# The down projection of a SwiGLU layer as seven block products, set between the gate and up products

## The chip, the cores and the metric

The kernel runs on one core of a Trainium2 chip. The metric is the device time of one execution in microseconds. The kernel before the change takes 1409.84 us, the median of 3 runs (1408.72 to 1411.44). It computes one layer of a transformer in float32: 1024 tokens, model width 1024, feed-forward width 2816.

## The reference

The layer is a causal stick-breaking attention with 16 heads of 64, beside it a cross attention of 4 heads over 256 memory rows, an output projection with residual, and then the part that the change touches:

```python
def rms_norm(x, g):
    xf = x.astype(jnp.float32)
    y = xf * lax.rsqrt(jnp.mean(xf * xf, axis=-1, keepdims=True) + EPS)
    return (y * g.astype(jnp.float32)).astype(x.dtype)

def swiglu(h, w_gate, w_up, w_down):
    return (jax.nn.silu(h @ w_gate) * (h @ w_up)) @ w_down
...
        x = x + jnp.concatenate([mix, cross], axis=-1) @ w_out[i]
        x = x + swiglu(rms_norm(x, ffn_norm[i]), w_gate[i], w_up[i], w_down[i])
```

The result must have float32's accuracy. TensorE reads float32 operands in a shortened form, so the kernel splits each operand into a high part (a copy in that form, name ending in h) and a low part (the operand minus its high part, name ending in l), and sums three matrix products: high by high, high by low, low by high. A "split" below is this pair: ScalarE writes the high part, another engine subtracts for the low part.

## The kernel before, in words

The feed-forward width is cut into 11 chunks of 256 (two blocks of 128, called fb). For a chunk the kernel computes gate and up, transposed, as 256 x 1024; then the block silu(gate) * up (called gu, also 256 x 1024, kept as four pieces of 128 x 512: fb by half of the tokens); then the product of gu with the chunk's 256 rows of w_down, which is added to the residual x2 (1024 x 1024, in SBUF for the whole stage).

Gate and up are already computed with seven block products each (Strassen's method in Winograd's form). Each such product is a `pe_product`: 12 matmuls of 128 x 512 output (4 blocks of the contracted width times 3 of the split), into PSUM banks 4 to 7. The sums of weight blocks that they need are made by GpSimd (`pool_sums`, four operations for each of gate and up), their high parts by ScalarE (`act_part_high`), their low parts by VectorE (`dve_part_low`). ScalarE copies products that are needed twice out of PSUM (`act_keep`), VectorE adds products (`dve_sum`) and forms the block from them (`dve_block`, with ScalarE's sigmoid before it).

The down product (`pe_down`) is done in the plain way: 8 token tiles by 2 column halves, for each 6 matmuls into one of the banks 0 to 3 in turn, and after each VectorE adds that bank to x2 (`dve_down`, 128 x 512). The 256 x 1024 rows of w_down arrive in two halves of 512 KB and are split by ScalarE and VectorE in operations of 128 x 1024 (`act_down_w`, `dve_down_w`). The gu block is split piece by piece (`act_block_high`, `dve_block_low`).

One pass of the program (`pe_body` and the functions of the same form for the other engines) computes the gate products of chunk c + 1, the down product of chunk c, and the up products of chunk c + 1. The first chunk's gate and up are made before, in the plain way (`pe_first`), and among them stand TensorE's transposes of the second half of the tokens (`pe_turn`, banks 0 and 1 in turn, copied out by `act_second` and `dve_second`). There are 10 passes: one written out, a loop with 4 turns of two, and one more written out. The last chunk's down product stands alone behind them. Nothing is scheduled by a planner: the order on each engine is the order of the calls in these functions, each engine runs its own in that order, and semaphores carry the dependencies.

Of the kernel before, what the change touches and what calls it, by code (L numbers as in the profile page):

```python
# [19 lines left out]
def trunk(nc, x, mem, norms, w_mem_kv, w_out, w_gate, w_up, w_down, sb_w_in, out):  # L20
# [35 lines left out]
    with ExitStack() as ctx:  # L56
# [22 lines left out]
        own = take("own", [P, BANK // 2 + 1], BF16, BANK + 2)  # L79
# [46 lines left out]
        pv_low = take("pv_low", [P, 2 * P])  # L126
        KB = 1024
        ex_at = cursor[0]
        cursor[0] += 14 * KB
        assert cursor[0] <= nc.sbuf_usable_end  # L130
# [46 lines left out]
        gu_h = at("gu_h", [P, FB, S], F32R, mk_at)  # L177
        gu_at = (x_at + 32 * KB - 2 * ROW, raw_at)
        gu_x = [at(f"gu_x{b}", [P, FB, S], F32, gu_at[b]) for b in range(2)]
        gu_l = [at(f"gu_l{b}", [P, FB, S], F32R, gu_at[b]) for b in range(2)]  # L180
# [22 lines left out]
        dw_at = (h_at, h_at + 16 * KB)  # L203
        dw_h = [at(f"dw_h{n}", [P, FB, BANK], F32R, dw_at[n]) for n in range(2)]
        dw_x = [at(f"dw_x{n}", [P, FB, BANK], F32, dw_at[n] + ROW) for n in range(2)]
        dw_l = [at(f"dw_l{n}", [P, FB, BANK], F32R, dw_at[n] + ROW) for n in range(2)]
# [427 lines left out]
        s_fd = [sem("down_w_left_loaded"), sem("down_w_right_loaded")]  # L634
        s_dh = sem("down_w_high_done")
        s_dl = sem("down_w_low_done")
# [447 lines left out]
        def act_first_high(act, half, fb):  # L1084
            n = 2 * half + fb
            act.wait_ge(s_bl, n + 1)
            c = slice(half * BANK, (half + 1) * BANK)
            act.activation(gu_h[:, fb, c], gu_x[0][:, fb, c], ACT.Copy).then_inc(s_gh, 1)

        def dve_first(dve, half, fb):  # L1090
            n = 2 * half + fb
            g = gu_x[0][:, fb, half * BANK:(half + 1) * BANK]
# [5 lines left out]

        def dve_first_low(dve, half, fb):
            n = 2 * half + fb  # L1100
            g = gu_x[0][:, fb, half * BANK:(half + 1) * BANK]
            c = slice(half * BANK, (half + 1) * BANK)
            dve.wait_ge(s_gh, n + 1)
            dve.tensor_tensor(gu_l[0][:, fb, c], g, gu_h[:, fb, c].bitcast(F32), ALU.subtract).then_inc(s_gl, 1)

# [69 lines left out]
        G0 = 8  # L1175
        DOWN_LAST = tuple(range(NT // 2, NT)) + tuple(range(NT // 2))
# [42 lines left out]
        def pool_sums(pool, c, m):  # L1219
# [9 lines left out]
            pool.tensor_tensor(a21, a11, a21, ALU.subtract).then_inc(s_sc, 1)  # L1229
            part_loaded(pool, c, m, 1)  # L1230
# [61 lines left out]
        def act_keep(act, c, m, i):  # L1292
# [31 lines left out]
        def dve_block(dve, c, m, par, i):  # L1324
            g, k = block_of(gu_x[par], i), kept[KEPT_OF[i]][:, :]
# [87 lines left out]
        def act_body(act, c, par, first=False, ahead=True):  # L1413
# [6 lines left out]
            if not first:  # L1420
                act_sigmoid(act, g, par1, 0)
# [538 lines left out]
```

## Time and profile before

| | |
|---|---|
| median of 3 runs | 1409.84 us |
| the profiled execution's own time | 1409.1 us |
| its span, first to last instruction | 1407.3 us |
| granted TensorE clock, mean | 0.993 |
| TensorE (PE) busy | 1365.0 us, 97% |
| VectorE (DVE) busy | 948.7 us, 67% |
| ScalarE (ACT) busy | 655.8 us, 47% |
| GpSimd (POOL) busy | 186.6 us, 13% |
| moved by DMA | 69.94 MB, mean 50 GB/s |

The profile is of one execution, whose span lies 1.8 us under its own device time. Matmul records overlap each other: a record lasts about 0.39 us, but the next matmul starts about 0.23 us after the one before. So TensorE's pace is read from start to start, or from the length of a stretch and the number of matmuls in it, not from the length of a record. VectorE's records overlap too: 128 x 512 operations of 0.69 us follow each other after 0.60 us. In the names, "x" is x2, "ps" is PSUM, L12 is line 12 of the kernel before.

### The profile page before, as it was taken

Reading aid. Unit: us, or ns where it says so; the run is one execution under the profiler, and the core shown is the slowest. Engines: PE = TensorE matmul, PEld = TensorE weight load, DVE = VectorE, ACT = ScalarE, POOL = GpSimd, SP = SyncE. Lnnn points to the kernel's source line nnn. Section 1 sums busy time; section 2 is a strip of 40 time slices with the busy share of each in tenths; the row PEclk is TensorE's granted clock in tenths of the full one; section 3 lists DMA queues with packets and bytes.
Section 4 is the critical chain, followed back from the end, with each engine's and each line's share of the span. In section 5 each row is a group of like instructions: output and inputs, shape, how many; then the busy total and the mean of one; then the engine's idle time right before and its main releaser. Section 6 shows DMA issues by size and latency. Waiting matters only on the chain. (4 is left out here: it accounts for less than half of the span.)

```text
span 1407.3 us, 20453 instructions
## 1 busy us (share of the span) xinstructions
PE 1365.0 (97%) x6974; PEld 1115.6 (79%) x6974; DVE 948.7 (67%) x1344; ACT 655.8 (47%) x1124; POOL 186.6 (13%) x155
## 2 busy tenths in 40 slices
PE   7999999999999999599999999999999999999999
PEld 4777888787888888488887788888888888888887
DVE  6677979788797978795257856556564555756455
ACT  7566666656666665762253422324133241322321
POOL 0000000000000000214015211202111121111200
PEclk9999999999999999799999999999999999999999
DMA  6100100101010011105111211111111111121103
GB/s 240 31 24 23 31 24 23 30 22 30 22 30 23 22 31 31 45 24 162 41 30 31 81 55 45 45 61 45 60 60 45 52 37 61 43 66 52 45 31 135
DMA packets 90118, 69.94 MB, mean 50 GB/s; under 512 B 3792, under 2 KB 75472, under 8 KB 90064
## 3 DMA queue, kind: packets, MB, share of 16 engines
q1 hardware_dynamic: 90064, 69.23, 15.9%
q8 instruction: 32, 0.52, 0.2%
q14 instruction: 22, 0.18, 0.0%
HBM read 65.03 MB, written 4.19 MB: 49 GB/s over the span
## 5 line engine op out<-in xcount | busy, mean ns | idle before, releaser
L1394 DVE TENSOR_TENSOR x<-ps,x 128x512 f32<-128x512 f32 x176 | 121.6, 691 | 71.2 <-PE ps L1384 67.0
L1300 ACT ACTIVATE kept<-ps 128x512 f32<-128x512 f32 x60 | 35.7, 595 | 235.4 <-PE ps L1288 235.4
L438 ACT ACTIVATE a_h<-ps 128x256 fp32r<-128x256 f32 (+2 forms) x96 | 78.0, 812 | 136.9 <-PE ps L353 136.9
L315 PE MATMUL ps<-hh,w_h 128*128 128x512 f32 x336 | 140.3, 417 | 0.0
L1384 PE MATMUL ps<-dw_h,gu_l 128*128 128x512 f32 x352 | 138.5, 394 | 0.0
L1384 PE MATMUL ps<-dw_l,gu_h 128*128 128x512 f32 x352 | 137.5, 391 | 0.0
L1384 PE MATMUL ps<-dw_h,gu_h 128*128 128x512 f32 x352 | 137.0, 389 | 0.3 <-issue 0.3
L315 PE MATMUL ps<-hh,w_l 128*128 128x512 f32 x336 | 132.4, 394 | 0.0
L315 PE MATMUL ps<-hl,w_h 128*128 128x512 f32 x336 | 131.9, 393 | 0.0
L1288 PE MATMUL ps<-ft_h,part_l 128*128 128x512 f32 x320 | 126.5, 395 | 0.0
L1288 PE MATMUL ps<-ft_l,part_h 128*128 128x512 f32 x320 | 125.2, 391 | 0.0
L1288 PE MATMUL ps<-ft_h,part_h 128*128 128x512 f32 x320 | 124.5, 389 | 0.0
L547 DVE TENSOR_TENSOR a_l<-ps,a_h 128x256 fp32r<-128x256 f32 (+2 forms) x96 | 91.6, 954 | 48.7 <-ACT a_h L438 48.1
L521 DVE TENSOR_TENSOR_SCAN fail<-fail,own 128x129 f32<-128x129 f32 (+3 forms) x128 | 107.8, 870 | 0.0
L1258 DVE TENSOR_TENSOR part_l<-part_x,part_h 128x512 fp32r<-128x512 f32 x140 | 94.4, 691 | 5.3 <-ACT part_h L1251 2.8
L534 DVE TENSOR_TENSOR succ<-fail,succ 128x256 f32<-128x256 f32 (+2 forms) x96 | 94.7, 987 | 0.3
L1288 PE MATMUL ps<-f_h,part_l 128*128 128x512 f32 x240 | 94.7, 395 | 0.0
L353 PE MATMUL ps<-ident,succ 128*128 128x128 f32 x576 | 81.4, 278 | 13.5 <-DVE a_l L547 8.6
L1288 PE MATMUL ps<-f_h,part_h 128*128 128x512 f32 x240 | 93.5, 390 | 0.6 <-DVE part_l L1258 0.6
L1288 PE MATMUL ps<-f_l,part_h 128*128 128x512 f32 x240 | 93.8, 391 | 0.0
L1312 DVE TENSOR_TENSOR kept<-ps,kept 128x512 f32<-128x512 f32 x30 | 20.8, 692 | 104.0 <-PE ps L1288 104.0
L554 POOL TENSOR_TENSOR o_t<-o_t,pv_low 128x256 f32 x24 | 23.7, 988 | 476.8 <-ACT o_t L450 476.8
(219 smaller groups left out, 3120.4 us busy)
## 6 DMA issues: line engine op xcount, KB each, us to landing
w_raw<-in_sb_w_in SPq DMA_DIRECT2D x52, 256.0 KB, 2.9
dw_x<-in_w_down SPq DMA_DIRECT2D x22, 512.0 KB, 3.3
part_x<-in_w_gate SPq DMA_DIRECT2D x40, 256.0 KB, 3.5
part_x<-in_w_up SPq DMA_DIRECT2D x40, 256.0 KB, 2.9
wo_raw<-in_w_out SPq DMA_DIRECT2D x20, 256.0 KB, 2.8
x_in<-in_x SPq DMA_DIRECT2D x8, 512.0 KB, 7.8
x<-in_x SPq DMA_DIRECT2D x16, 256.0 KB, 6.0
out<-x SPq DMA_DIRECT2D x16, 256.0 KB, 2.0
```

The lines of the kernel that those rows point to most:

```text
L315: mm = pe.matmul(j_ps[:, 0], w[:, kc // 4, kc % 4], h[:, kc, half * BANK:(half + 1) * BANK], start=(kc == 0 and i == 0), stop=(kc == KC - ...
L353: mm = pe.transpose(t_ps[:, h, j * P:(j + 1) * P], succ[:, u % 2, h, j * P:(j + 1) * P], ident[:, :])
L438: act.activation(a_h[:, :, 0:w // P, col * P:(col + 1) * P], t_ps[:, :, 0:w].rearrange("p h (j q) -> p h j q", q=P), ACT.Copy).then_inc(s_ ...
L521: dve.tensor_tensor_scan(back, back, own[:, BANK - w:BANK + 1][:, ::-1], 0.0, ALU.mult, ALU.max).then_inc(s_scan, 1)
L534: done = dve.tensor_tensor(g, f[:, :, 1:w + 1], g, ALU.mult)
L547: dve.tensor_tensor(a_l[:, :, 0:w // P, c], t_ps[:, :, 0:w].rearrange("p h (j q) -> p h j q", q=P), a_h[:, :, 0:w // P, c].bitcast(F32), A ...
L554: pool.tensor_tensor(both, both, pv_low[:, :], ALU.add).then_inc(s_o, 1)
L1258: dve.tensor_tensor(part_l[m][p][:, :, :].rearrange(flat), part_x[m][p][:, :, :].rearrange(flat), part_h[p][:, :, :].rearrange(flat).bitca ...
L1288: mm = pe.matmul(product_bank(m, p), w[:, k], g[:, k], start=(p in (0, 1, 3) and k == 0 and i == 0), stop=(k == 3 and i == 2), skip_group_ ...
L1300: act.activation(kept[i][:, :], product_bank(m, (0, 2, 3)[i]), ACT.Copy).then_inc(s_kp, 1)
L1384: mm = pe.matmul(ps[:, (2, 3, 0, 1)[d % 4]], g[:, fb, t * P:(t + 1) * P], w[n][:, fb], start=(fb == 0 and i == 0), stop=(fb == FB - 1 and ...
L1394: dve.tensor_tensor(o, ps[:, (2, 3, 0, 1)[d % 4]], o, ALU.add).then_inc(s_x2, 1)
```

## The change

Each down product except the last chunk's becomes seven block products of the same method. With A the transposed gu block (its pieces A11, A12, A21, A22) and B the chunk's rows of w_down (pieces B11 to B22 of 128 x 512), product k is one of seven combinations of A times one of seven combinations of B: 4 token tiles by 3 of the split, 12 matmuls, each tile into a bank of its own, banks 0 to 3. The products accumulate in the banks, and start anew at k = 0, 4 and 5. After each one VectorE adds all four banks to a quarter of x2 in one operation of 128 x 4 x 512 (`dve_down`), and TensorE may not begin the next one before that add is done.

The seven stand between the 14 gate and up products, one behind every second. GpSimd makes the sums of A (`pool_a_sum`, four) and of B (`pool_b_sum`, four) and the seven low parts of B (`pool_b_low`); ScalarE makes 14 high parts (`act_a_high`, `act_b_high`), VectorE seven low parts of A (`dve_a_low`), each 128 x 512. High and low parts lie in rings of two. w_down arrives in four pieces of 256 KB for each chunk. `pool_sums` is cut, its last sum now stands apart (`pool_last_sum`).

The last chunk keeps the plain way (`pe_last`), now with eight banks in turn. Silu keeps its two steps (gate times sigmoid before, times up afterwards). The transposes among the first chunk's products rotate through banks 0 to 3 (`turn_ps`, `wait_turn_bank`). The diff, cut to what the text speaks of:

```diff
+            if g >= XU0 + KC:
+                return ps[:, (g - XU0 - KC) % 4]
-            if g >= XU0:
+            if g in (XU0 + KC + 2, XU0 + KC + 3):
+                pe.wait_ge(s_x2, X0)
+            elif g >= XU0 + KC + 4:
+                pe.wait_ge(s_xl, g - 3)
+            elif g >= XU0:
                 pe.wait_ge(s_xl, g - 1)
...
+        A_OPS = (A11, "S2", "S3", "A22", "A12", S1, S4)
+        B_OPS = ("B11", "B11", "B12", "B12", "B21", "B11", "B22")
+        C_OF = ((0, 0), (0, 1), (1, 1), (1, 0), (0, 0), (1, 1), (0, 1))
+
+        def ring_free(act, c, k):
+
+            if k >= 2 or not (isinstance(c, int) and c == 0):
+                act.wait_ge(s_dn, down_done(c, k - 2) if k >= 2 else down_done(c - 1, k + 5))
+
+        def act_a_high(act, c, par, k):
+            ring_free(act, c, k)
+            if k in (0, 3, 4):
+                act.wait_ge(s_bl, block_done(c, {0: 0, 3: 1, 4: 3}[k]))
+            else:
+                act.wait_ge(s_as, 4 * c + {1: 2, 2: 3, 5: 1, 6: 4}[k])
+            act.activation(ah[(par + k) % 2][:, :], ax[a_slot(par, A_OPS[k])][:, :], ACT.Copy).then_inc(s_gh, 1)
+
+        def a_low(par, k):
+            return al[a_slot(par, A_OPS[k]) if k else "low of A11"]
+
+        def dve_a_low(dve, c, par, k):
+
+            dve.wait_ge(s_gh, 7 * c + k + 1)
+            if 0 < k < 6:
+                dve.wait_ge(s_as, 4 * c + (0, 4, 3, 1, 4, 2)[k])
+            slot = a_slot(par, A_OPS[k])
+            dve.tensor_tensor(a_low(par, k)[:, :], ax[slot][:, :], ah[(par + k) % 2][:, :].bitcast(F32), ALU.subtract
+                              ).then_inc(s_gl, 1)
+
+            if n == 0:
+                pool.wait_ge(s_bd["B12"], 16 * c + 16)
+                pool.wait_ge(s_bd["B22"], 16 * c + 16)
+                pool.tensor_tensor(b12, b22, b12, ALU.subtract).then_inc(s_bs, 1)
+            elif n == 1:
+                pool.wait_ge(s_bs, 4 * c + 1)
+                pool.wait_ge(s_bw, 7 * c + 1)
+                pool.tensor_tensor(b11, b12, b11, ALU.add).then_inc(s_bs, 1)
...
+        def pool_b_low(pool, c, par, k):
+            pool.wait_ge(s_bh, 7 * c + k + 1)
+            pool.tensor_tensor(bl[(par + k) % 2][:, :], bx[B_OPS[k]][:, :], bh[(par + k) % 2][:, :].bitcast(F32),
+                               ALU.subtract).then_inc(s_bw, 1)
+
+        def pe_down(pe, c, par, k):
+
+            pe.wait_ge(s_gl, 7 * c + k + 1)
+            pe.wait_ge(s_bw, 7 * c + k + 1)
+            h, l = ah[(par + k) % 2], a_low(par, k)
+            wh, wl_ = bh[(par + k) % 2], bl[(par + k) % 2]
+            pe.wait_ge(s_x2, X0 + 7 * c + k)
+            for t in range(4):
+                for i, (g, w) in enumerate(((h, wh), (h, wl_), (l, wh))):
+                    mm = pe.matmul(ps[:, t], g[:, t * P:(t + 1) * P], w[:, :], start=(k in (0, 4, 5) and i == 0),
+                                   stop=(i == 2), skip_group_check=True)
+            mm.then_inc(s_dn, 1)
+
+        def dve_down(dve, c, k):
+            half, n = C_OF[k]
+            d = 7 * c + k
+            dve.wait_ge(s_dn, d + 2)
+            dve.wait_ge(s_x2, X0 if isinstance(c, int) and c == 0 and k < 2 else X0 + d - 1)
+            o = x2[:, 4 * half:4 * half + 4, n * BANK:(n + 1) * BANK]
+            dve.tensor_tensor(o, ps[:, 0:4], o, ALU.add).then_inc(s_x2, 1)
+
+
...
-            for p in range(7):
-                pe_product(pe, c + 1, 0, p)
-            pe_down(pe, c, par)
-            for p in range(7):
-                pe_product(pe, c + 1, 1, p)
+            after = (1, 3, 5, 7, 9, 11, 13)
+            for n in range(14):
+                pe_product(pe, c + 1, n // 7, n % 7)
+                if n in after:
+                    pe_down(pe, c, par, after.index(n))
+
+        def pool_body(pool, c, par, ahead=True):
+            pool_a_sum(pool, c, par, 3)
+            pool_b_low(pool, c, par, 1)
+            pool_b_low(pool, c, par, 2)
+            pool_b_sum(pool, c, 2)
+            pool_b_sum(pool, c, 3)
+            pool_sums(pool, c + 1, 1)
+            pool_b_low(pool, c, par, 3)
+            pool_last_sum(pool, c + 1, 1)
+            for k in (4, 5, 6):
+                pool_b_low(pool, c, par, k)
+            if ahead:
+                pool_sums(pool, c + 2, 0)
+                pool_b_sum(pool, c + 1, 0)
+                pool_b_low(pool, c + 1, 1 - par, 0)
+                pool_last_sum(pool, c + 2, 0)
+                pool_b_sum(pool, c + 1, 1)
+                for n in range(3):
+                    pool_a_sum(pool, c + 1, 1 - par, n)
 
...
```

**What moves, in the engines' order.** TensorE in the first pass before the change, at the end of the seventh gate product (L1288) and the start of the down product (L1384); part_h and part_l are parts of the gate weights, dw_h and dw_l of w_down, gu_h and gu_l of the block:

```order
L1288 MATMUL ps<-ft_h4_153,part_h6_192 128x512
L1288 MATMUL ps<-ft_l4_157,part_h6_192 128x512
L1288 MATMUL ps<-ft_h4_153,part_l06_178 128x512
L1384 MATMUL ps<-dw_h0_193,gu_h_139 128x512
L1384 MATMUL ps<-dw_l0_197,gu_h_139 128x512
L1384 MATMUL ps<-dw_h0_193,gu_l0_142 128x512
```

TensorE in the first pass after the change, at the end of the second gate product (L1298) and the first down product (L1478), whose rows repeat four times; bh and bl are parts of B, ah of A:

```order
L1298 MATMUL ps<-f_h0_130,part_h1_202 128x512
L1298 MATMUL ps<-f_l0_132,part_h1_202 128x512
L1298 MATMUL ps<-f_h0_130,part_l01_188 128x512
L1478 MATMUL ps<-bh0_212,ah0_157 128x512
L1478 MATMUL ps<-bl0_214,ah0_157 128x512
L1478 MATMUL ps<-bh0_212,al_low of A11_156 128x512
```

The down product has moved from behind seven gate products to behind the second, and there are 12 of its matmuls there where 96 stood in one piece.

VectorE in the loop before the change, at the last gate piece and the first adds of the down product (L1394); kept0 and kept1 are products copied out of PSUM:

```order
L1328 TENSOR_TENSOR gu_x0_140<-gu_x0_140,kept1_200 128x512
L1255 REGISTER_ALU
L1258 TENSOR_TENSOR part_l11_180<-part_x11_166,part_h1_187 128x512
L1327 REGISTER_ALU
L1328 TENSOR_TENSOR gu_x0_140<-ps,kept0_199 128x512
L1391 ISA
L1392 REGISTER_ALU
L1394 TENSOR_TENSOR x2_124<-ps,x2_124 128x512
L1255 REGISTER_ALU
L1258 TENSOR_TENSOR part_l12_181<-part_x12_167,part_h2_188 128x512
L1391 REGISTER_ALU
L1394 TENSOR_TENSOR x2_124<-ps,x2_124 128x512
L1255 REGISTER_ALU
```

VectorE in the first pass after the change, from the add of down product 0 to that of product 1 (L1488); A22 here holds S2, one of the sums of A, and the rows at L1389 are low parts of A:

```order
L1488 TENSOR_TENSOR x2_124<-ps,x2_124 128x4x512
L1389 TENSOR_TENSOR A22_152<-A22_143,ah1_158 128x512
L1268 TENSOR_TENSOR part_l04_191<-part_x04_177,part_h4_205 128x512
L1268 TENSOR_TENSOR part_l05_192<-part_x05_178,part_h5_206 128x512
L1334 TENSOR_TENSOR ax_A11_139<-ps,kept0_228 128x512
L1268 TENSOR_TENSOR part_l06_193<-part_x06_179,part_h6_207 128x512
L1350 TENSOR_TENSOR ax_A11_139<-ax_A11_139,kept0_228 128x512
L1389 TENSOR_TENSOR al_A21_149<-ax_A21_140,ah0_157 128x512
L1488 TENSOR_TENSOR x2_124<-ps,x2_124 128x4x512
```

Between two adds of a bank stood at most one other operation; now two adds of four banks have seven operations between them, six of which read no PSUM (in the loop the first of them stands ahead of the first add).

GpSimd in the loop before the change, the four sums for the up weights:

```order
L1224 ISA
L1225 TENSOR_TENSOR part_x13_168<-part_x14_169,part_x16_171 128x512
L1198 REGISTER_ALU
L1227 ISA
L1228 TENSOR_TENSOR part_x12_167<-part_x13_168,part_x10_165 128x512
L1229 TENSOR_TENSOR part_x14_169<-part_x10_165,part_x14_169 128x512
L1231 REGISTER_ALU
L1236 TENSOR_TENSOR part_x15_170<-part_x11_166,part_x12_167 128x512
```

GpSimd in the loop after the change, from the low part of B's product 1 to the sums for the up weights (part_x12 to part_x14):

```order
L1466 TENSOR_TENSOR bl1_215<-bx_B11_208,bh1_213 128x512
L1465 REGISTER_ALU
L1466 TENSOR_TENSOR bl0_214<-bx_B12_209,bh0_212 128x512
L1449 TENSOR_TENSOR bx_B12_209<-bx_B21_210,bx_B11_208 128x512
L1451 REGISTER_ALU
L1452 TENSOR_TENSOR bx_B11_208<-bx_B22_211,bx_B11_208 128x512
L1231 REGISTER_ALU
L1232 TENSOR_TENSOR part_x13_183<-part_x14_184,part_x16_186 128x512
L1234 REGISTER_ALU
L1235 TENSOR_TENSOR part_x12_182<-part_x13_183,part_x10_180 128x512
L1236 TENSOR_TENSOR part_x14_184<-part_x10_180,part_x14_184 128x512
```

The up sums stand behind four operations for the down product that were not on this engine; a pass holds 23 operations where it held 8.

## Rows read from the trace of the kernel before

**Rows 1.** The chain that ended last, in order of time: start us, us, what.

```profile
771.97 1.25 POOL part_x L1229
...
775.09 19.64 PE ps L1288 x84
794.73 22.19 PE ps L1384 x96
816.91 38.62 PE ps L1288 x168
855.54 21.77 PE ps L1384 x96
...
1381.39 0.30 issue
1381.69 22.44 PE ps L1384 x96
```

**Rows 2.** PE's waits from 690 us on: line, released by, us in total, times, longest.

```profile
PE ps L719 <- DVE ft_x L1129: 2.0, 1, 2.0
PE ps L1288 <- DVE part_l L1258: 0.6, 1, 0.6
```

**Rows 3.** Busy us (instructions) by stretch: length, PE PEld DVE ACT POOL, granted clock.

```profile
998.52:1119.72 121.20, 121.20 (x529) 99.12 (x529) 69.42 (x100) 35.80 (x60) 20.62 (x16) 1.00 0.17 52
775.09:1381.39 606.30, 606.30 (x2640) 495.63 (x2640) 353.59 (x503) 180.79 (x301) 99.44 (x76) 1.00 0.17 51
```

**Rows 4.** Groups of two passes (998.52 to 1119.72 us): busy us, mean ns; idle before.

```profile
L1394 DVE TENSOR_TENSOR x<-ps,x 128x512 f32<-128x512 f32 x32 | 22.1, 691 | 12.4 <-PE ps L1384 11.6
L1258 DVE TENSOR_TENSOR part_l<-part_x,part_h 128x512 fp32r<-128x512 f32 x28 | 18.7, 684 | 0.6 <-ACT part_h L1251 0.6
L1251 ACT ACTIVATE part_h<-part_x 128x512 fp32r<-128x512 f32 x28 | 16.0, 621 | 2.4 <-POOL part_x L1228 2.4
L1225 POOL TENSOR_TENSOR part_x<-part_x,part_x 128x512 f32<-128x512 f32 x4 | 5.2, 1296 | 93.9 <-PE ps L1288 93.9
```

**Rows 5.** Timeline of VectorE, 1133 to 1141 us: start us, us.

```profile
1133.58 0.69 DVE L1312 TENSOR_TENSOR kept<-ps,kept 128x512 f32<-128x512 f32 x1 [5.31 <-PE ps L1288]
1134.31 1.04 DVE L1335 TENSOR_TENSOR gu_x<-kept,gu_x 128x512 f32<-128x512 f32 x1
...
1138.73 1.88 DVE L1258 TENSOR_TENSOR part_l<-part_x,part_h 128x512 fp32r<-128x512 f32 x3
```

**Rows 6.** Timeline of GpSimd, the same stretch.

```profile
1133.51 1.29 POOL L1229 TENSOR_TENSOR part_x<-part_x,part_x 128x512 f32<-128x512 f32 x1
```

**Rows 7.** Timeline of VectorE from 786 us on.

```profile
786.89 2.32 DVE L1368 TENSOR_TENSOR dw_l<-dw_x,dw_h 128x1024 fp32r<-128x1024 f32 x1
```

**Rows 8.** Timeline of GpSimd, the same stretch.

```profile
788.26 2.09 POOL L1228 TENSOR_TENSOR part_x<-part_x,part_x 128x512 f32<-128x512 f32 x1
```

**Rows 9.** The 128x2048 add, timeline of VectorE.

```profile
764.96 2.29 DVE L1154 TENSOR_TENSOR f<-f,ft_x 128x2048 f32<-128x2048 f32 x1 [1.19 <-POOL f L1148]
```

**Rows 10.** GpSimd's in-place sums at L1148: ns least, median, longest.

```profile
L1148 POOL TENSOR_TENSOR f<-f,f x4: 1318/2556/3352, 755.3 to 761.6; 128x512 f32<-128x512 f32 x4
```

**Rows 11.** The page's DMA issues: KB each, median us to landing.

```profile
part_x<-in_w_up SPq DMA_DIRECT2D x40, 256.0 KB, 2.9
```

**Rows 12.** Timeline of PE among the first chunk's products.

```profile
740.59 0.66 PE L719 MATMUL ps<-ident,xn 128*128 128x128 f32 x4 [0.47 <-DVE ft_x L1126]
...
742.25 0.40 PE L1068 MATMUL ps<-f_h,gw_l 128*128 128x512 f32 x1
744.60 1.11 PE L719 MATMUL ps<-ident,xn 128*128 128x128 f32 x4 [1.96 <-DVE ft_x L1129]
...
748.03 0.39 PE L1068 MATMUL ps<-f_h,gw_h 128*128 128x512 f32 x1
```

**Rows 13.** The granted clock behind the second wait, columns as in Rows 3.

```profile
744.60:748.00 3.40, 3.40 (x10) 2.89 (x11) 3.37 (x6) 0.69 (x1) 0.00 (x0) 0.50 0.00 0
```

**Rows 14.** Timeline of GpSimd before the first pass.

```profile
768.99 1.28 POOL L1225 TENSOR_TENSOR part_x<-part_x,part_x 128x512 f32<-128x512 f32 x1 [4.06 <-DMA part_x<-in_w_gate]
```

More of the change, by code:

```diff
@@ L1371, in pe_down, with block_done @@
-        def pe_down(pe, c, par, last=False):
+        def block_done(c, i):
+            return (1, 4, 3, 2)[i] if isinstance(c, int) and c == 0 else blocks(c, 1, i + 1)
+        A_OPS = (A11, "S2", "S3", "A22", "A12", S1, S4)
[4 more added lines that the diff above has]
+                act.wait_ge(s_dn, down_done(c, k - 2) if k >= 2 else down_done(c - 1, k + 5))
@@ L1382, in pe_down @@
[L1382 to L1392 removed]
+                    pe.wait_ge(s_gl, 7 * LAST + 3)
+                elif d == NT // 2:
+                    pe.wait_ge(s_gl, 7 * LAST + 4)
@@ new lines, in pe_last @@
+                if d == 3:
+                    pe.wait_ge(s_bl, blocks(LAST, 1, 4))
+                elif d > 3:
+                    pe.wait_ge(s_x2, X0 + DN * LAST + max(0, d - 7))
+                for fb in range(FB):
+                    i = BLOCKS.index((fb, half))
+                    h, l = last_ah[i], al[a_slot(0, (A11, "A22", A21, "A12")[i])]
+                    for j, (g, w) in enumerate(((h, last_bh), (h, last_bl), (l, last_bh))):
+                        mm = pe.matmul(last_bank(d), g[:, q], w[n][fb][:, :],
+                                       start=(fb == 0 and j == 0), stop=(fb == FB - 1 and j == 2))
@@ L1393, in dve_down, with dve_last @@
+                mm.then_inc(s_dn, 1)
+        def dve_last(dve, d):
+            n, t = d // NT, DOWN_LAST[d % NT]
+            dve.wait_ge(s_dn, DN * LAST + d + 2)
+            dve.wait_ge(s_x2, X0 + DN * LAST)
             o = x2[:, t, n * BANK:(n + 1) * BANK]
-            dve.tensor_tensor(o, ps[:, (2, 3, 0, 1)[d % 4]], o, ALU.add).then_inc(s_x2, 1)
+            dve.tensor_tensor(o, last_bank(d), o, ALU.add).then_inc(s_x2, 1)
         def sp_body(sp, c, ahead=True):
-            for n in (2, 3, 0, 1):
+            first = isinstance(c, int) and c == 0
+            for n in (2, 3):
@@ L1444, in act_body @@
                     act_part_high(act, g + 1, 0, p)
-            for i in range(1, 4):
-                act_block_high(act, g, par1, i)
+                act_b_high(act, g, par1, 0)
+                act_a_high(act, g, par1, 0)
         def dve_body(dve, c, par, first=False, ahead=True):
@@ L1720, in _ @@
             act_body(act, FC - 2, 1, ahead=False)
-            act_down_w(act, FC - 1, 1)
+            act_last_a(act, 0)
+            act_last_a(act, 1)
+            act_last_b(act, 0, 0)
+            act_last_a(act, 2)
+            act_last_b(act, 0, 1)
+            act_last_a(act, 3)
+            for fb in range(FB):
+                act_last_b(act, 1, fb)
         @block.vector
@@ L1849, in _ @@
             for d in range(2 * NT):
[L1850 to L1852 removed]
+                dve_last(dve, d)
         @block.tensor
```

334 lines of the change are left out of this document (204 added, 130 removed).

## The prediction, made before the changed kernel had run

> **What bounds the kernel now.** First the chain of waits: from 775.09 us to the end it is TensorE alone, in a strict pattern: 96 matmuls of the down product in 21.77 or 22.19 us, then 168 gate and up matmuls, ten times, and the last chunk's 96 at the end [rows 1]. Then PE's waits: after 690 us there are two worth a word, 2.0 and 0.6 us, both ahead of the first pass; inside the passes none [rows 2]. Then busy time by stretch: the ten passes take 606.30 us and hold 2640 matmuls, so 0.2297 us each and 60.63 us a pass, at clock 1.00; over two passes VectorE is busy 69.42 of 121.20 us, ScalarE 35.80, GpSimd 20.62 [rows 3]. The passes cost what their matmuls cost. So a matmul less is worth 0.23 us as long as the other engines, which get more work, stay in time.
>
> **The matmuls.** A down product has 7 x 12 = 84 instead of 96: 12 less in each of ten passes, 120 x 0.2297 = 27.6 us off. The new ones have the shape of the old. Between the two lengths of the old down product the pace differs by 0.0044 us, 0.4 us a pass in either direction; I take the mean. The new pass is 252 x 0.2297 = 57.9 us. I call the gate and up products P0 to P13 and the down products D0 to D6; each is 12 matmuls, 2.76 us, in the order P0 P1 D0 P2 P3 D1 P4 P5 D2 P6 P7 D3 and so on.
>
> **The load of the others, per pass.** VectorE loses 16 adds at 0.691, four low parts of 0.69 and two of 1.2 us, and gets seven low parts and seven adds of 2048 columns. The trace has no such add out of PSUM. One of 512 columns out of PSUM takes 0.691 us, as long as one within SBUF (0.684), and one of 2048 columns within SBUF 2.29 [rows 4, 9]; three low parts in a row take 1.88, so 0.60 from start to start [rows 5]. Ends: 2.2 (the same 0.09 overlapped) and 2.4 (four times 0.60); I take 2.29, the row of its size. Sum: 34.7 - 11.1 - 2.8 - 2.4 + 4.8 + 16.0 = 39 of 57.9 us. ScalarE loses two of 1.06 and four of 0.63 and gets 14 of 0.62: 22 us. GpSimd goes from 8 to 23 operations of 1.30: 30 us [rows 3, 4]. w_down comes in pieces of 256 KB; such a piece lands in 2.9 us [rows 11], and each is asked for when its buffer's last low part is made, 8 us or more before its use; SP's queue holds nothing that waits longer than these. Cost nothing; were one late, GpSimd's sum behind it would be late by as much.
>
> **What the engines cost each other.** At 1134.31 VectorE begins a product of two SBUF tiles while GpSimd runs from 1133.51 to 1134.80; it takes 1.04 us instead of 0.69, ending 0.55 us after GpSimd did. The add out of PSUM at 1133.58 under the same GpSimd operation takes its plain 0.69 [rows 5, 6]. The other way round, GpSimd's sum at 788.26 takes 2.09 us, with VectorE in a low part until 789.21 [rows 7, 8]. So a GpSimd operation and a VectorE operation with two SBUF inputs exclude each other for their whole length; PSUM operands are free of it.
> The Trainium skill has this as a rule (SBUF — State Buffer, section on SBUF's two separate sides): the pair of ports is an exclusive lock, and the loser blocks fully. By this rule, the trace agrees (1.04 for 0.69 us). It speaks against this change, which nearly triples GpSimd's operations; the sum by it is the 1384 below; if the two only shared bandwidth, there would be no queueing in the passes, and it would be 1381.
> In a pass 27 VectorE operations have two SBUF inputs (14 + 7 low parts, 6 block steps): 27 x 0.60 = 16 us, beside GpSimd's 30: 46 of 57.9 us, if never idle together. It fits, so only a local rush can stall TensorE.
>
> **Where it is tight.** TensorE may start Dk when the add of D(k-1) is done, 5.5 us after it ended; the add takes 2.3, so VectorE may be 3.2 us late. The worst place is D2. From the end of D0 to the start of D2 TensorE has P2 P3 D1 P4 P5, 13.8 us. VectorE has in that time, in this order: the add of D0 (2.2), two part_l, a sum, part_l, a block step, a low part of A (six times 0.60), then the add of D1 (2.3): 8.1 us. GpSimd has there two sums of B and the three up sums, which may start at the end of P3; five operations of 1.3 us, 6.5 us, and I find nearly each of them ahead of one waiting VectorE operation. 8.1 + 6.5 = 14.6, less what GpSimd does under the first add and the sum, about 1.1, plus hand-overs between engines of some 0.05 us each: 13.9 to 14.2. So D2 is 0.1 to 0.4 us late; I take 0.3. Ends: 0 (GpSimd finds its gaps) and 1.7 us (nothing overlaps, eight hand-overs of 0.1). The other places, walked the same way, keep over 1.8 us (D0 of the next pass, behind the three A sums) or over 2 us (D3, P6, P7). Ten passes: 3 us, ends 0 and 17.
>
> **Ahead of the first pass.** Two transposes of the second half wait for a bank, 0.47 and 1.96 us [rows 2, 12], and the matmuls behind the second run at clock 0.50, the lower level of 1.2 GHz, after that idle time, until 748.03 [rows 12, 13]: one group of transposes and six matmuls in 3.4 us where 1.9 would do. With four banks both waits go: 0.5 + 2.1 + 1.5 = 4.1 us. What is late next is P0: it waited 0.57 us already on the low part of the first gate weights, whose DMAs wait for GpSimd's f sums, and these for the last of the same transposes. So that chain moves up too. GpSimd's new low part of B falls into its 4.06 us wait for the DMA [rows 14], VectorE's low part of 2048 columns now stands ahead of the first part_l and may cost some tenths. I take 3.8 off; ends 0 and 4.1.
> In the first pass D1 needs all four sums of A and two of B, and these the last block, 1.4 us into P0: seven GpSimd operations (9.1), VectorE's three part_l and one operation of 2048 columns between them (4), ScalarE's high part (0.6): 15.1 us, against 13.8: 1.3 late. The backlog makes D2 late again, about 1.5. 2.8 us on, ends 0 and 5.
>
> **The end.** D6 now stands behind the last up product, so the last block's split hides behind it: the 0.3 us gap ahead of the last 96 matmuls goes [rows 1]; these stay.
>
> **Sum**, against the profiled execution's 1409.1 us (span 1407.3 and 1.8 around it): 1409.1 - 27.6 - 3.8 + 2.8 + 3.0 - 0.3 = 1383.2. The median of the runs is 0.7 above that execution: **1384 us**.
>
> **Rivals.**
> (a) No stalls in the passes, and a full gain ahead of them: 1409.8 - 27.6 - 4.1 - 0.3 = 1378. For it: VectorE and GpSimd have a fifth of the time spare even if they exclude each other. Against: three up sums start just as VectorE has its densest row.
> (b) The rush at D2 costs the upper end, 1.7 us a pass: 1384 + 14 = 1398. For it: GpSimd's four in-place sums under VectorE's load had a median of 2.56 and up to 3.35 us instead of 1.32 [rows 10].
> (c) Slower. The same queueing, one step on: with GpSimd's operations at the 2.45 us which they average there, 23 fill 56 of 57.9 us, GpSimd's order becomes the pace and D2 waits as long as the transposes did, 2.1 us, and pulls the clock down once a pass, 1.5 us more. With 0.4 us for the pace behind it, 4.0 x 10 - 27.6 - 1.3 = +11: 1421. It decides from 2.9 us of stall a pass on (27.6 + 1.3 over ten). Against: the waits are bounded by the other's length, and VectorE's two-SBUF work is 16 us of 58, not the dense row of 2048-column operations as there.
> (d) The matmuls themselves go slower: each bank gets only three at a time, where the old down product put six into one. At 0.26 us for the 84, 2.5 us a pass come back: 1409. Against: the gate and up products add across products too, and run at 38.62/168 = 0.2299 [rows 1].
>
> **Chances.** Forecast 0.52, (a) 0.25, (b) 0.14, (c) 0.06, (d) 0.03. A change within 0.2% (2.8 us) can't be told from none here. Faster 0.91, the same 0.03, slower 0.06. The range reaches from (a) to just past (b): 1377 to 1400, with (c), (d) and a little beyond outside, some 1 in 7.
>
> **What would show it.** In the profile after: 252 matmuls a pass and a pass of 57.9 to 58.5 us; PE's waits on the down line, released by VectorE's add, at D2 before any other; no wait at the transposes and no stretch at 0.50; GpSimd near 30 us busy a pass (well above 35 would be (b) or (c)); the four-bank add at 2.3 us. It is wrong if PE's waits per pass exceed 1.7 us, if another semaphore (a DMA of w_down, a high part) ends them, or if the pace of the matmuls changes.

## The result and the profile after

| | before | after |
|---|---|---|
| median of the runs, us | 1409.64 (1408.72 to 1411.44) | 1386.13 (1384.76 to 1387.05) |
| ratio, 95% interval | | 0.9831 (0.9814 to 0.9848) |
| profiled execution: time, span, us | 1409.1, 1407.3 | 1385.98, 1384.2 |
| first to last product of the first chunk (to P0), us | 52.45 | 52.07 |
| P0 to the last 96 matmuls, us | 606.60 | 581.97 |

The kernel is 23.5 us faster; forecast were 1384 us and a range of 1377 to 1400. The last two lines are start times of PE's timeline taken from each other. Together they are 25.0 us shorter. The part ahead of them, whose code did not change but for the places of two small tiles (tested below), took 1.8 us longer in this execution: the first chunk's products start at 724.47 us, 722.64 before, and between 722.6 and 725.7 over all the kernels below. That is why small effects are read below from these two stretches beside the medians.

The page of the changed kernel, busy time by engine and the group of the new add:

```profile
PE 1339.9 (97%) x6854; PEld 1094.1 (79%) x6854; DVE 1083.0 (78%) x1262; ACT 689.2 (50%) x1206; POOL 424.1 (31%) x309
L1488 DVE TENSOR_TENSOR x<-ps,x 128x2048 f32<-128x2048 f32 x70 | 160.1, 2287 | 71.4 <-PE ps L1478 71.3
```

Its chain of waits, in order of time (start us, us, what), which answers to [rows 1]: the down product (L1478) is now 12 matmuls between pairs of gate and up products (L1298). Where some 2.7 us are missing between two rows of 24, a down product stood.

```profile
1011.17 5.55 PE ps L1298 x24
1016.71 2.77 PE ps L1478 x12
1019.49 5.55 PE ps L1298 x24
1027.77 5.50 PE ps L1298 x24
...
1358.67 22.36 PE ps L1533 x96
```

Busy time by stretch, columns as in [rows 3]: from D2 of the first pass to the end of the passes, all ten passes, and two passes in the middle.

```profile
801.36:1358.51 557.15, 557.15 (x2425) 455.23 (x2426) 461.77 (x409) 205.62 (x368) 309.38 (x215) 1.00 0.18 53
776.54:1358.51 581.97, 579.69 (x2522) 473.03 (x2521) 484.38 (x423) 216.61 (x386) 332.61 (x228) 1.00 0.18 54
1000.08:1115.98 115.90, 115.90 (x506) 94.71 (x505) 97.04 (x85) 42.45 (x76) 66.99 (x47) 1.00 0.18 54
```

From 801.36 us on PE is busy all the time, at clock 1.00; a pass takes 57.95 us. In it VectorE is busy 48.5 us, ScalarE 21.2, GpSimd 33.5. PE's waits after 690 us, answering to [rows 2]:

```profile
PE ps L1087 <- DVE ft_x L1134: 2.9, 1, 2.9
PE ps L1478 <- POOL bl L1466: 2.3, 1, 2.3
```

The first is new, in the first chunk. The second is D2 of the first pass. It starts at 801.36 us, 0.15 us after the add of D1 has ended, on which it waits (timeline of VectorE):

```profile
798.93 2.28 DVE L1488 TENSOR_TENSOR x<-ps,x 128x2048 f32<-128x2048 f32 x1
```

The low part that the view names, made at the same time, is the one for D3; in the kernels below the same wait stands with the add.

The place that was walked in the prediction, from the add of D0 to that of D1, here in a pass in the middle; timeline of VectorE, then GpSimd:

```profile
1019.61 2.29 DVE L1488 TENSOR_TENSOR x<-ps,x 128x2048 f32<-128x2048 f32 x1 [1.56 <-PE ps L1478]
1021.82 3.50 DVE L1268 TENSOR_TENSOR part_l<-part_x,part_h 128x512 fp32r<-128x512 f32 x2
1025.24 0.68 DVE L1334 TENSOR_TENSOR ax_A<-ps,kept 128x512 f32<-128x512 f32 x1
1025.85 1.18 DVE L1268 TENSOR_TENSOR part_l<-part_x,part_h 128x512 fp32r<-128x512 f32 x1
1026.95 1.78 DVE L1350 TENSOR_TENSOR ax_A<-ax_A,kept 128x512 f32<-128x512 f32 x1
1028.65 1.79 DVE L1389 TENSOR_TENSOR al_A<-ax_A,ah 128x512 fp32r<-128x512 f32 x1
1030.37 2.28 DVE L1488 TENSOR_TENSOR x<-ps,x 128x2048 f32<-128x2048 f32 x1
```

```profile
1021.78 1.29 POOL L1449 TENSOR_TENSOR bx_B<-bx_B,bx_B 128x512 f32<-128x512 f32 x1 [0.17 <-POOL bl L1466]
1023.16 1.61 POOL L1452 TENSOR_TENSOR bx_B<-bx_B,bx_B 128x512 f32<-128x512 f32 x1
1025.12 1.36 POOL L1232 TENSOR_TENSOR part_x<-part_x,part_x 128x512 f32<-128x512 f32 x1 [0.35 <-PE ps L1298]
1026.56 1.62 POOL L1235 TENSOR_TENSOR part_x<-part_x,part_x 128x512 f32<-128x512 f32 x1
1028.14 1.75 POOL L1236 TENSOR_TENSOR part_x<-part_x,part_x 128x512 f32<-128x512 f32 x1
```

Every VectorE operation with two SBUF inputs here is held until the GpSimd operation in progress has ended (1.2 to 1.8 us instead of 0.68, 3.50 instead of 1.29 for the two at 1021.82); the one that reads PSUM at 1025.24 keeps its 0.68, the two adds their 2.29. D2 starts at 1033.11, 0.5 us after the add has ended: it keeps up, with little to spare.

### The profile page after: what moved, and what is told of

It is laid out like the page before. It is cut to its first block, busy times and chain, and to the rows that moved or that the text cites. A ratio compares the mean times of both kernels' runs of the same rounds, so it can differ in the third digit from the quotient of the medians.

```text
span 1384.2 us, 20643 instructions
## 1 busy us (share of the span) xinstructions
PE 1339.9 (97%) x6854; PEld 1094.1 (79%) x6854; DVE 1083.0 (78%) x1262; ACT 689.2 (50%) x1206; POOL 424.1 (31%) x309
## 4 chain that ended last, share of the span: by engine, by line
PE 91%; ACT 3%; DVE 3%; POOL 2%; issue 1%; DMA 0%; SPq 0%; ACTq 0%; POOLq 0%; DVEq 0%
PE ps L1298 27%; PE ps L326 17%; PE ps L1478 14%; PE ps L1010 7%; PE ps L380 5%; PE ps L364 5%; PE ps L354 4%; PE ps L295 3%; PE ps L1087 2%; PE ps L1533 2%; PE ps L798 1%; ACT junk L703 1%; PE ps L938 1%; PE ps L902 0%; PE ps L738 0%
## 5 line engine op out<-in xcount | busy, mean ns | idle before, releaser
L1488 DVE TENSOR_TENSOR x<-ps,x 128x2048 f32<-128x2048 f32 x70 | 160.1, 2287 | 71.4 <-PE ps L1478 71.3
L1466 POOL TENSOR_TENSOR bl<-bx_B,bh 128x512 fp32r<-128x512 f32 x70 | 96.6, 1380 | 200.5 <-ACT bh L1462 200.5
L1268 DVE TENSOR_TENSOR part_l<-part_x,part_h 128x512 fp32r<-128x512 f32 x140 | 140.5, 1033 | 2.5 <-POOL part_x L1236 2.5
L558 DVE TENSOR_TENSOR a_l<-ps,a_h 128x256 fp32r<-128x256 f32 (+2 forms) x96 | 91.5, 953 | 48.9 <-ACT a_h L449 48.5
L1298 PE MATMUL ps<-ft_h,part_l 128*128 128x512 f32 x320 | 126.5, 395 | 0.0
L1298 PE MATMUL ps<-ft_l,part_h 128*128 128x512 f32 x320 | 125.2, 391 | 0.0
L1298 PE MATMUL ps<-ft_h,part_h 128*128 128x512 f32 x320 | 124.5, 389 | 0.0
L1478 PE MATMUL ps<-bh,ah 128*128 128x512 f32 x280 | 109.1, 390 | 2.3 <-POOL bl L1466 2.3
L1478 PE MATMUL ps<-bl,ah 128*128 128x512 f32 x280 | 109.5, 391 | 0.0
L364 PE MATMUL ps<-ident,succ 128*128 128x128 f32 x576 | 82.0, 279 | 13.3 <-DVE a_l L558 8.6
L1298 PE MATMUL ps<-f_h,part_l 128*128 128x512 f32 x240 | 94.7, 395 | 0.0
L1261 ACT ACTIVATE part_h<-part_x 128x512 fp32r<-128x512 f32 x140 | 82.9, 621 | 22.9 <-POOL part_x L1235 14.2
L1298 PE MATMUL ps<-f_l,part_h 128*128 128x512 f32 x240 | 93.9, 391 | 0.0
L1298 PE MATMUL ps<-f_h,part_h 128*128 128x512 f32 x240 | 93.4, 389 | 0.0
```

The costliest lines, as they stand in the source:

```text
L364: mm = pe.transpose(t_ps[:, h, j * P:(j + 1) * P], succ[:, u % 2, h, j * P:(j + 1) * P], ident[:, :])
L558: dve.tensor_tensor(a_l[:, :, 0:w // P, c], t_ps[:, :, 0:w].rearrange("p h (j q) -> p h j q", q=P), a_h[:, :, 0:w // P, c].bitcast(F32), A ...
L1261: act.activation(part_h[p][:, :, :].rearrange(flat), part_x[m][p][:, :, :].rearrange(flat), ACT.Copy).then_inc(s_fh, 1)
L1268: dve.tensor_tensor(part_l[m][p][:, :, :].rearrange(flat), part_x[m][p][:, :, :].rearrange(flat), part_h[p][:, :, :].rearrange(flat).bitca ...
L1298: mm = pe.matmul(product_bank(m, p), w[:, k], g[:, k], start=(p in (0, 1, 3) and k == 0 and i == 0), stop=(k == 3 and i == 2), skip_group_ ...
L1466: pool.tensor_tensor(bl[(par + k) % 2][:, :], bx[B_OPS[k]][:, :], bh[(par + k) % 2][:, :].bitcast(F32), ALU.subtract).then_inc(s_bw, 1)
```

## The experiments

Times are medians; the kernel before, on the same chips, had 1409.6. "Chunk" is from the first chunk's first product to P0, "passes" from P0 to the last 96 matmuls, each in the profiled execution; "turns" are the transposes of the second half of the tokens.

| kernel | us (ratio to before, 95%) | chunk | passes | sum |
|---|---|---|---|---|
| before | 1409.6 | 52.45 | 606.60 | 659.05 |
| after | 1386.13 (0.981 to 0.985) | 52.07 | 581.97 | 634.04 |
| before, turns in four banks | 1412.95 (1.0014 to 1.0036) | 55.53 | 606.49 | 662.02 |
| before, two tiles moved | 1410.08 (0.9993 to 1.0012) | 52.43 | 606.60 | 659.03 |
| after, turns in two banks | 1385.97 (0.9822 to 0.9849) | 50.63 | 582.21 | 632.84 |
| after, sums late | 1386.29 (0.9821 to 0.9848) | 50.89 | 583.77 | 634.66 |
| after, f sums wait | 1387.99 (0.9832 to 0.9862) | 54.03 | 582.20 | 636.23 |
| after, four adds | 1387.86 (0.9829 to 0.9856) | 51.89 | 582.15 | 634.04 |
| after, one more | 1388.24 (0.9830 to 0.9862) | 52.07 | 583.53 | 635.60 |
| after, three more | 1395.52 (0.9882 to 0.9915) | 52.04 | 591.02 | 643.06 |
| after, 12 matmuls back | 1410.74 (1.0000 to 1.0018) | 53.25 | 608.19 | 661.44 |
| after, up sums late | 1385.44 (0.9817 to 0.9844) | 52.06 | 580.96 | 633.02 |
| after, three edits | 1383.45 (0.9805 to 0.9831) | 49.06 | 582.87 | 631.93 |

**Is the gain the matmuls?** Down product 0 of each pass is made twice:

```diff
-            for t in range(4):
+            for t in (0, 1, 2, 3, 0, 1, 2, 3) if k == 0 else range(4):
```

> The 12 matmuls of down product 0 are made twice in each of the ten passes (the second time over the first), so a down product has 96 matmuls again in the new order. Theory (the gain of the change is the 120 matmuls, at 0.2297 us each): 27.6 us come back, less what of the 2.4 us wait of the first pass the later D1 and D2 hide: 1411.3 to 1413.7. Rival (a part of the gain is the new order or the four banks at once): under 1410.

1410.74: the gain is gone, though the median lies under the range of the theory and over that of the rival. The two stretches are 27.4 us longer for 120 matmuls. The wait at D2 of the first pass is 1.2 us shorter (1.1 for 2.3), as PE's waits of this kernel show:

```profile
PE ps L1478 <- DVE x L1488: 1.1, 1, 1.1
```

And the low clock behind the wait of the first chunk holds for six more matmuls, 1.2 us longer. So the new order, the adds of four banks and three matmuls at a time in a bank are worth nothing by themselves: with 96 matmuls they leave the stretches 2.4 us longer than before, by the waits of the chunk and of the first pass.

**Where the data lie.** Two tiles of an earlier stage change places in SBUF in the kernel before, as in the changed kernel.

> The kernel before, with only the two small tiles own and pv_low at their new places in SBUF. In the changed kernel's trace the first matmul of the first chunk starts at 724.47 us, in the kernel before at 722.64. Theory 1 (that 1.8 us is the spread between executions): 1409.6 within 1 us, that start anywhere from 722 to 725. Theory 2 (the places of the tiles cost it): 1411.4 and a start near 724.5.

Nothing, to 0.1%. In this kernel the first chunk's products start at 723.93 us, where they started at 722.64 before and at 724.47 after: inside the spread, as the first theory had it.

**The transposes.** Only the four banks, on the kernel before; and the changed kernel with the two banks of before:

```diff
+            if g >= XU0 + KC:
+                return ps[:, (g - XU0 - KC) % 4]
...
-            if g >= XU0:
+            if g in (XU0 + KC + 2, XU0 + KC + 3):
+                pe.wait_ge(s_x2, X0)
+            elif g >= XU0 + KC + 4:
+                pe.wait_ge(s_xl, g - 3)
+            elif g >= XU0:
```

> The kernel before, with only the four banks for the eight transposes among the first chunk's products. Theory 1 (what stalls TensorE there is VectorE's chain that copies the eight tiles out, and more banks only move the wait to the first product that needs all of them, the first matmul of the second half): the two waits at the transposes (0.5 and 2.0 us) go, a wait of 1.5 to 3 us with matmuls at clock 0.50 behind it appears on the first chunk's own matmuls, released by VectorE; the time is 0 to 1.5 us under the kernel before. Theory 2 (my prediction's step: the banks are what is waited for): no such wait, 3.8 us less, 1405.8.

> The changed kernel, with the transposes back in two banks in turn. Theory 1: the wait of 2.9 us on the first chunk's matmuls turns back into one of about 2 us at the transposes; the time is within 1 us of the changed kernel's 1386.1. Theory 2: 3.8 us more, 1390.

Alone on the kernel before, the four banks make it slower, 3.1 us in the chunk and 3.4 by the medians; in the changed kernel they cost 1.4 us in the chunk, which the medians don't show. The waits at the transposes do go in both. PE's waits after 690 us with the four banks alone:

```profile
PE ps L1074 <- DVE ft_x L1135: 5.9, 1, 5.9
PE ps L1390 <- issue: 0.3, 1, 0.3
```

PE has only run ahead: the first product of the second half needs all eight transposes copied out by VectorE. And the earlier last transpose releases GpSimd's eight f sums, which now run beside VectorE's copies. In the changed kernel (timelines of VectorE, GpSimd and PE) three of VectorE's four sums take 1.55 us instead of 0.69, then PE starts, and at the lower clock:

```profile
745.06 0.69 DVE L1137 TENSOR_TENSOR ft_x<-ft_x,f 128x512 f32<-128x512 f32 x1
...
747.11 1.55 DVE L1137 TENSOR_TENSOR ft_x<-ft_x,f 128x512 f32<-128x512 f32 x1
```

```profile
746.82 5.89 POOL L1149 TENSOR_TENSOR f<-f_h,f_l 128x512 f32<-128x512 f32 x4 [28.82 <-PE ps L738]
```

```profile
753.06 0.77 PE L1087 MATMUL ps<-f_h,gw_h 128*128 128x512 f32 x1 [2.87 <-DVE ft_x L1134]
753.62 0.63 PE L1087 MATMUL ps<-f_l,gw_h 128*128 128x512 f32 x1
```

```profile
753.06:756.54 3.48, 3.48 (x8) 2.80 (x9) 1.50 (x2) 2.02 (x2) 3.48 (x3) 0.51 0.02 5
```

With two banks in the changed kernel these f sums start 1.5 us later, counted from the chunk's first product, and the second waiting transpose waits 0.60 us where it waited 1.96 before [rows 12]. What the traces show as the reason is another part of the change: before, ScalarE's high part of the first block stood between these copies and waited 2.80 us for VectorE, and VectorE's low part of it (0.69 us) stood between them too; now both stand behind them. No run moves these two alone. ScalarE's timeline before:

```profile
741.89 0.63 ACT L1088 ACTIVATE gu_h<-gu_x 128x512 fp32r<-128x512 f32 x1 [2.80 <-DVE gu_x L1097]
```

PE's waits of the changed kernel with two banks:

```profile
PE ps L1292 <- DVE part_l L1262: 1.4, 1, 1.4
PE ps L732 <- DVE ft_x L1128: 0.6, 1, 0.6
PE ps L732 <- DVE ft_x L1125: 0.5, 1, 0.5
```

**Is it the holding?** The f sums wait until VectorE is done, nothing else:

```diff
             pool.wait_ge(s_xt, XU0 + 2 * KC)
+            pool.wait_ge(s_ts, 4)
```

> GpSimd's eight f sums begin only when VectorE has made the last of its four sums of the second half; no more. Theory (with four banks the transposes end sooner, GpSimd's sums begin sooner and hold VectorE's three sums at 1.55 us instead of 0.69): PE's wait ahead of the first product of the second half falls from 2.9 us to 0.5 or less, without a stretch at the lower clock behind it; but GpSimd's sums begin some 5 us later, so the first gate weights come later and P0 starts 52 to 55 us behind the first product of the first chunk (52.1 in the changed kernel): 1386 to 1389. Rival (VectorE's queue of evictions is simply that long): the wait stays over 2 us, and the same time.

The four sums take 0.69 us again; PE's wait falls from 2.87 to 1.13 us, no matmul behind it is slow, and P0 waits 5.1 us instead, with twelve slow matmuls behind:

```profile
PE ps L1299 <- DVE part_l L1269: 5.1, 1, 5.1
PE ps L1087 <- DVE ft_x L1134: 1.1, 1, 1.1
```

So 1.7 us of the wait were the holding (the two of the three held sums that stand ahead of the last copy, 0.87 each) and 1.1 are VectorE's queue. My bound of 0.5 was too low; that the loss only changes its place came as expected. Taking the four sums together behind the copies does the same more gently:

```diff
-                dve.wait_ge(s_xl, XU0 + KC + c + 1)
-                dve.tensor_tensor(ft_x[2][:, k], ft_x[3][:, k], f11[:, k], ALU.add).then_inc(s_ts, 1)
...
+            dve.wait_ge(s_xl, XU0 + 2 * KC)
+            dve.tensor_tensor(ft_x[2][:, :, :].rearrange(flat), ft_x[3][:, :, :].rearrange(flat),
+                              f11[:, :, :].rearrange(flat), ALU.add).then_inc(s_ts, 4)
```

> The changed kernel, with VectorE's four sums of the f blocks (128x512 each, between the copies of the last four transposes, three of them held up to 1.55 us by GpSimd) put behind the last copy as one operation of 128x2048. Theory 1 (VectorE's chain, lengthened by its port conflict with GpSimd, is what TensorE waits for): the chain ends 4 us sooner, the wait of 2.9 us and the slow matmuls behind it go, 4.5 us; P0 then waits for its own low part, at about 774.2 where it started at 776.5, so 2.3 us stay; the stall at D2 of the first pass may take some of it. 1384 (1382 to 1386). Rival (the first pass is set by GpSimd's chain of seven sums, wherever P0 starts): the wait goes but D2 of the first pass is later by as much, 1386.

PE's wait ahead of the second half is gone, P0 waits 3.4 us, the wait at D2 of the first pass stays at 2.3 us, and slow matmuls follow it (last section): no gain.

**The add of four banks.** As four adds of 512 columns with one signal:

```diff
-            dve.tensor_tensor(o, ps[:, 0:4], o, ALU.add).then_inc(s_x2, 1)
+            for t in range(4):
+                add = dve.tensor_tensor(o[:, t], ps[:, t], o[:, t], ALU.add)
+            add.then_inc(s_x2, 1)
```

> The changed kernel, with each add of four banks as four adds of 128x512, one signal behind the last. Theory (VectorE's adds out of PSUM follow each other after 0.60 us, so 2.49 instead of 2.29 us; two of them lie ahead of D2, whose slack is 0.46 us of which about 0.15 is the hand-over): the slack at D2 goes to 0.1 or to a stall of 0.1 us per pass; 0 to 2 us more than the changed kernel, 1387. Rival (the adds of one tile wait for each other, 0.69 each, 2.76): D2 is late by 0.6 us in each pass, 1392.

2.48 us instead of 2.29; the slack ahead of D2 is 0.3 instead of 0.5, and the stretches are the same. The medians lie 1.7 us apart, with overlapping runs; the profile has no place for it.

**More work for GpSimd.** Its low part for down product 2 is made once, or three times, more:

```diff
+            for i in range(1 if k == 2 else 0):
+                if i:
+                    pool.wait_ge(s_again, 1 * c + i)
+                pool.tensor_tensor(bl[(par + k) % 2][:, :], bx[B_OPS[k]][:, :], bh[(par + k) % 2][:, :].bitcast(F32),
+                                   ALU.subtract).then_inc(s_again, 1)
+            if k == 2:
+                pool.wait_ge(s_again, 1 * c + 1)
...
```

> The changed kernel, with one GpSimd operation of 128x512 more in each pass: the low part of B's combination 2 is made twice, between the end of D0 and the start of D2, where VectorE is densest. Theory 1 (GpSimd's and VectorE's two-input operations exclude each other, and D2 has 0.3 us of slack left): the operation takes 1.3 us, GpSimd's idle time ahead of the up sums takes up to 0.4 of it, so D2 is late by 0.6 to 1.0 us in each of nine passes and 1.3 more in the first: 1392 to 1396. Rival (GpSimd is busy 33 of 58 us, so one more is free): 1386.

> The same with three GpSimd operations more at that place in each pass. Theory 1: D2 is late by 3.9 less about 0.7, so 3.2 us a pass, and where TensorE idles so long its clock falls to 0.50 for a while, up to 1.5 us more: 32 to 47 us more than the changed kernel, 1418 to 1433, slower than the kernel before. If the clock holds it is the lower figure. Rival (free as long as GpSimd has time): under 1390.

Both cost far less than I had expected. With one more, D2 still has 0.6 us of slack in every later pass, and what this kernel costs in its stretches, 1.6 us, are slow matmuls behind D2 of the first pass (last section). VectorE's row between the adds, to hold against the one above:

```profile
1024.30 3.41 DVE L1269 TENSOR_TENSOR part_l<-part_x,part_h 128x512 fp32r<-128x512 f32 x2
1027.63 0.68 DVE L1335 TENSOR_TENSOR ax_A<-ps,kept 128x512 f32<-128x512 f32 x1
1028.23 1.18 DVE L1269 TENSOR_TENSOR part_l<-part_x,part_h 128x512 fp32r<-128x512 f32 x1
1029.34 1.77 DVE L1351 TENSOR_TENSOR ax_A<-ax_A,kept 128x512 f32<-128x512 f32 x1
1031.03 1.78 DVE L1390 TENSOR_TENSOR al_A<-ax_A,ah 128x512 fp32r<-128x512 f32 x1
```

It is held by the same amounts, and so it is with three more (3.41, 1.18, 1.77 and 1.78 us). GpSimd and VectorE take turns: an operation waits for the one in progress, not for those queued behind it, so a row of five is held at most five times by the rest of one GpSimd operation, however many there are. What more GpSimd work does is to last longer. With three more it reaches into VectorE's next row, ahead of the add of D2, and D3 is late in every pass, by some 0.6 us (it starts 8.93 us behind D2 instead of 8.32), which with the slow first matmul behind each wait makes 7 of the 9 us that this kernel costs in its stretches; the rest are again slow matmuls behind D2 of the first pass:

```profile
1039.72 1.78 DVE L1390 TENSOR_TENSOR S<-S,ah 128x512 fp32r<-128x512 f32 x1
1041.42 3.52 DVE L1269 TENSOR_TENSOR part_l<-part_x,part_h 128x512 fp32r<-128x512 f32 x2
```

```profile
PE ps L1486 <- DVE x L1496: 7.1, 11, 2.3
```

**The up sums out of the row.** GpSimd's low part for down product 3 goes first:

```diff
+            pool_b_low(pool, c, par, 3)
             pool_sums(pool, c + 1, 1)
-            pool_b_low(pool, c, par, 3)
```

> In each pass GpSimd's three sums for the up weights stand behind its low part for down product 3 instead of ahead of it, so that none of them runs beside VectorE's row of two-SBUF operations between the adds of D0 and D1. Theory (GpSimd's sums and VectorE's two-SBUF operations hold each other): D2 of the first pass is 0.3 to 1.2 us late instead of 2.4, the slack ahead of D2 in the later passes grows from 0.5 to 2.5 us or more, 1.8 us gained: 1384.2, 1383 to 1385.5. Rival 1 (the backlog of sums of A and B alone makes D2 of the first pass late): still over 2 us late, 1386. Rival 2 (the up sums now come too late for the low parts ahead of the add of D2): D3 is late in every pass, up to 0.6 us each, 1388 to 1392.

Behind its first two low parts (3.49 us, beside the sums of B) VectorE's row runs freely, here in a pass in the middle:

```profile
1024.30 0.68 DVE L1268 TENSOR_TENSOR part_l<-part_x,part_h 128x512 fp32r<-128x512 f32 x1
1025.08 0.69 DVE L1350 TENSOR_TENSOR ax_A<-ax_A,kept 128x512 f32<-128x512 f32 x1
1025.69 0.68 DVE L1389 TENSOR_TENSOR al_A<-ax_A,ah 128x512 fp32r<-128x512 f32 x1
```

The slack ahead of D2 grows from 0.5 to 2.9 us, and D2 of the first pass is 0.2 us late instead of 2.4. But half of that moves to D3 of the first pass, 1.1 us late now: the sums hold VectorE in its next row, ahead of the add of D2. The only wait that the view of PE's waits still shows in the passes is this one:

```profile
PE ps L1478 <- DVE x L1488: 0.9, 1, 0.9
```

The passes gain 1.0 us, not 1.8; the medians, 0.7 apart, can't tell it. The theory has the place right and the sum too high; the second rival is right in the first pass alone.

**Together.** Two banks for the transposes, the up sums late, and VectorE's 2048-column low part of the third f sum behind the low part of the first gate weights:

```diff
             dve_first(dve, 1, 0)
+            dve_part_low(dve, 1, 0, 0)
             dve_f_low(dve, 3)
-            dve_part_low(dve, 1, 0, 0)
```

> The changed kernel with three edits: the transposes of the second half rotate through two banks again, the up sums stand behind the low part for down product 3, and VectorE's 2048-column low part of the third f sum stands behind the low part of the first gate weights. Theory: 1.4 us for the transposes (the span of the first chunk with two banks), 0 to 1.4 us for P0's own wait, as GpSimd's gate sums are held once less, and 1.8 us in the first pass: 1381.5 to 1384. Rival (these waits only move to the next late operation): 1385 to 1386.5.

1383.45 us, 2.7 under the changed kernel (1382.43 to 1385.04 against 1384.76 to 1387.05, overlapping by 0.3), and 2.1 us less in the two stretches: the best of the kernels here. P0 waits for nothing, but P1 0.7, D1 1.0 and D3 0.9 us. Of the 3.0 us taken away ahead of the first pass 1.9 come back in the passes (582.87 against 580.96 with the up sums late alone). D1 is released by a low part of A, and the sums of A hang on the first chunk's last block.

## Why the prediction was right, and where not

- **The matmuls, −27.6 us.** Right: 252 a pass in 57.95 us, and the 120 put back cost 27.4. The pace is 0.2300 us, within the 0.4 us a pass allowed; rival (d) falls.
- **The four-bank add, 2.29 us.** Measured 2.287; the row of its size was the right one.
- **The load.** ScalarE 21.2 (22 worked out) and GpSimd 33.5 (30 plus its being held). VectorE 48.5 instead of 39: the prediction counted its work, and the time in which it is held is shown as busy: most of the other 9.5 us.
- **Stalls at D2, +3.0 us.** Wrong: none in nine passes. The place was right (0.5 us is the least slack of all), the size was not. The walk gave 13.9 to 14.2 us: 8.1 of work, 5.4 held, 0.4 to 0.7 for hand-overs. From D0's end at 1019.33 to the add's end at 1032.65 it took 13.3, of 13.8 that there are: 8.1 of work, 2.2 + 0.5 + 1.1 + 1.1 = 4.9 held, and 0.3 for all else, so that most hand-overs lie inside the holding. What failed are two terms, each by 0.1 to 0.5 us: the held time, by the step that puts nearly each GpSimd operation whole ahead of a VectorE one, and the hand-overs counted on top of it. The forecast had D2 0.3 us late in each of ten passes, and that is the 3 us. By the same step the added operations, and rivals (b) and (c), were priced too high: with three more operations a pass the kernel is still 14 us faster than before. The Trainium skill's rule of the exclusive lock (SBUF — State Buffer, section on SBUF's two separate sides) agrees with this trace, as the 1.78 us for 0.68 show; my reading of it as a queue was too dear.
- **Ahead of the first pass, −3.8 us.** Wrong: −0.4. Both waits went, as said, but "what is late next is P0" is the step that failed: late next is the first product of the second half, which needs VectorE's eight copies. PE idles there for 2.87 us and has the low clock behind it, and GpSimd, released earlier, adds 1.7 of these. With the transposes left alone the rest of the change brings 1.8 us here (50.63 us for the chunk instead of 52.45), as far as the traces show by the first block's high and low part moved from between the copies, which I did not see.
- **The first pass, +2.8 us.** Its sum was right (2.6), its parts were not: D1 0.2 late for 1.3, D2 2.4 for 1.5. That it stems from the holding, and not from the backlog of sums of A and B alone, is shown by the kernel with the up sums late (0.2 at D2).
- **The end, −0.3 us.** Right: the chain has no gap ahead of the last 96.

In the two stretches −25.9 us were forecast and −25.0 came: two errors of about 3 us, one of each sign. That they cancel is luck, and the forecast is nearer to the result than its steps were. The rest up to the 1386 measured is the 1.8 us ahead of them, which the runs give no cause but their spread.

## What to carry to other kernels

- To weigh two engines that exclude each other, count the operations of the one that is waited for: each is held by at most the rest of one operation of the other. More work on the other side costs only when it reaches into the next row.
- A wait taken from an engine ahead of a join is worth what the join's other arm leaves. Ask who makes the last operand of the join, and whom the earlier finish sets going beside that maker.
- Where PE is busy all the time, fewer matmuls are worth their full length, here 27.4 us of 27.6. Look for cheaper arithmetic before better order.

## What the runs showed of the hardware

Equal waits were followed by different clocks. In the first pass PE waits 2.3 us for D2 in five of these kernels, with nearly the same work around it. In the changed kernel the 12 matmuls of D2 then run at 0.23 us each, clock 1.00 (the upper level, 2.4 GHz); in the kernel with one more operation the first nine take 3.72 us, most of them 0.43 each, at a mean clock of 0.54, near the lower level of 1.2 GHz:

```profile
801.36:804.21 2.85, 2.85 (x12) 2.33 (x13) 2.15 (x4) 1.16 (x2) 1.28 (x2) 1.00 0.00 0
```

```profile
802.26:805.98 3.72, 3.72 (x9) 2.90 (x10) 3.02 (x4) 1.15 (x2) 3.00 (x3) 0.54 0.00 0
```

That is 1.6 us, as much as all that this kernel costs more in its stretches. Eight or so are slow there with three more operations and with the sums late too, none with the transposes in two banks; and behind the one wait of 2.9 us in the first chunk between 7 and 13 matmuls are slow, with the same code. What decides it stays open: the runs don't show it. A cost of a microsecond that rests on a clock's dip needs more than one profile.
